# Down projections of a two-layer decoder step: activation sums made in the up projections and streamed, contraction split by even and odd blocks

## The chip, the cores and the metric

The kernel runs on one core of one Trainium2 chip. The metric is the device time of one execution in microseconds (us), the median of several runs. Instructions go to five engines: TensorE (PE, its weight loads PEld), VectorE (DVE), ScalarE (ACT), GpSimd (POOL) and SyncE (SP, whose queue SPq issues nearly all DMAs).

## The reference, cut to what matters

Two layers, each a mixer followed by a SwiGLU feed-forward block with a residual and a LayerNorm; 1088 tokens (1024 of a prompt, 64 samples), all in float32. The part that the change touches:

```python
D_MODEL = 1024; D_FF = 2816
def swiglu(x, w_gu, w_down):
    gate, up = jnp.split(x @ w_gu, 2, axis=-1)
    return (jax.nn.silu(gate) * up) @ w_down
# in each layer
x = layer_norm(ALPHA * x + swiglu(x, w_gu, w_down), g, b)
```

## The kernel before, in words

Every float32 product is made of three matmuls of rounded parts: ACT casts an operand to its high part, DVE subtracts to get the low part, and PE multiplies high by high, high by low and low by high.

**Up projection, `ffn_up`.** `KF` = 22 iterations `j`, one for each block of 128 of the 2816 hidden channels. Each iteration makes seven products of a 2x2 block scheme (`PRODUCTS`), in two halves of 272 tokens. The weights of `j + 1` need four sums ("T sums", `make_t_sums`, L2179), which POOL makes first in iteration `j`; ACT casts them (`w_part`) and DVE makes the low parts. After the fourth product (`S_T2`) ACT must copy the PSUM bank away (`take`, L2251), before PE may start the fifth, `S_T3`, which uses the same bank. ACT's order within an iteration is written out by hand: copy of the first product, casts of B11 and B21, the SiLU of the first gate, casts of T1 and T2, `take` of `S_T2`, and so on. POOL ends an iteration with the two products that give the activations: `u3` (tokens from 544) and `u2` (tokens 0 to 543). SP stores both to `scratch_a` (L2196, L2198), and then issues the two 512 KB weight loads of `j + 2` (L2187).

**Down projection, `ffn_down`.** The 22 blocks are cut into a first and a second half of 11 (`KH2`), the prompt's tokens into two halves of 512, the 1024 outputs into two of 512. Seven products `p` of 11 steps `k` each (77 steps `n`); a step multiplies one 128x512 activation operand by one 128x512 weight operand with 12 matmuls (4 token tiles by 3 parts), and in products 0, 1, 4 and 5 two more for the sample tokens. `FACTOR_A` and `FACTOR_B` say which sums are the operands: 5 of 7 products have a sum of two activation blocks, 5 of 7 a sum of two weight blocks. All activations are held on chip in `aT`. POOL makes all weight sums (L2524); the activation sums (L2533) are made by POOL, or by DVE in every second step where both are sums. Operands pass through rings: `RW` = 3 raw weights, `RS` = 2 activation sums, `RB` = 5 high and low parts. DVE also adds each finished tile of PSUM into the residual `X` (`take`, L2776 and L2780), for product `p - 1` after step 3 of product `p`, and does the LayerNorm's vector part. PE may use a PSUM bank again only when that add is done. In layer 0 the result is also transposed on PE for the next projection (L2635).

Both projections run twice: tiles `ffn0u`, `ffn0d` in layer 0, `ffn1u`, `ffn1d` in layer 1.

Of the kernel before, what the change touches and what calls it, by code (L numbers as in the profile page):

```python
# [2113 lines left out]

def ffn_up(nc, st, w, tag, q, side):
    S_B11, S_B21, S_T1, S_T2, S_T3, S_T4, S_B22 = range(7)
    X_A11, X_A12, X_S1, X_S2, X_S3, X_A22, X_S4 = range(7)
    w_v = w.rearrange("(k p) n -> p k n", p=P)
    with ExitStack() as ctx:
# [12 lines left out]
        x1, sg2 = sb("x1", [P, HALF_T]), sb("sg2", [P, HALF_T])  # L2132
        ps = ctx.enter_context(nc.psum_tensor(f"{tag}_ps", [P, 6, 512], F32))
# [4 lines left out]
        xhi_done, xlo_done = [sem(f"xhi{o}") for o in range(7)], [sem(f"xlo{o}") for o in range(7)]  # L2138
        s1_made, s2_made, s3_made, s4_made = (sem(n) for n in ("s1_made", "s2_made", "s3_made", "s4_made"))
# [40 lines left out]

        with nc.Block() as block:
# [51 lines left out]
            def _(act):  # L2233
# [46 lines left out]
                for j in range(KF):  # L2280
# [127 lines left out]
    return a_out[1]  # L2408


def ffn_down(nc, st, A, l, tag, aT, XT, y_out, a_out):
    KH2, HT, HN, RB, RW, RS, TAIL = KF // 2, SEQ // 2, D // 2, 5, 3, 2, 3
    S_BANK, UP_FREE = 7, 7
    A11, A12, A21, A22 = (0, 0), (0, 1), (1, 0), (1, 1)
    B11, B12, B21, B22 = (0, 0), (0, 1), (1, 0), (1, 1)
# [20 lines left out]
    a_sum_steps = [n for n in range(STEPS) if len(FACTOR_A[n // KH2]) > 1]  # L2436
    a_sum_at = {n: r for r, n in enumerate(a_sum_steps)}

    def dve_sums_a(n):
        return n in a_sum_at and n in w_sum_at and n % KH2 % 2 == 0  # L2440

    a_sum_count, made = {}, {True: 0, False: 0}
    for n in a_sum_steps:
        made[dve_sums_a(n)] += 1
        a_sum_count[n] = made[dve_sums_a(n)]
# [24 lines left out]
    with ExitStack() as ctx:  # L2470
        sb = lambda n, s, d=F32: ctx.enter_context(nc.sbuf_tensor(f"{tag}_{n}", s, d))
        sem = lambda n: st.sem(f"{tag}_{n}")
        X, raw, a_sum = sb("X", [P, TILES, D]), sb("w", [P, RW, HN]), sb("a_sum", [P, RS, HT])
# [8 lines left out]
        a11_in = [sem(f"a11_in{k}") for k in range(KH2)]  # L2482
        GROUPS12, GROUPS2 = [(0, 2), (2, 5), (5, 8), (8, 11)], [(0, 4), (4, 8), (8, 11)]
        a12_in, a22_in, a21_in = ([sem(f"{n}_in{g}") for g in range(len(gs))] for n, gs in
                                  (("a12", GROUPS12), ("a22", GROUPS2), ("a21", GROUPS2)))
        s_in = [sem(f"s_in{h}") for h in range(2)]
        x_first, x_right, x_left0, x_left1, x_sample = (sem(n) for n in ("x_first", "x_right", "x_left0", "x_left1", "x_sample"))
        w_sum_done, a_sum_pool, a_sum_dve = sem("w_sum_done"), sem("a_sum_pool"), sem("a_sum_dve")
# [5 lines left out]
        def a_block(ab, k):  # L2494
            h, kh = ab
            return aT[:, kh * KH2 + k, HT * h:HT * h + HT]

        def b22(k):
            return aT[:, k, HT:SEQ]

        def group_sem(sems, groups, k):
            return next(sems[g] for g, (k0, k1) in enumerate(groups) if k0 <= k < k1)

        def wait_block(eng, ab, k):
            if ab == A11:
                eng.wait_ge(a11_in[k], 16)
            elif ab == A12:
                eng.wait_ge(group_sem(a12_in, GROUPS12, k), 16)
            elif ab == A22:
                eng.wait_ge(group_sem(a22_in, GROUPS2, k), 16)  # L2510
            else:
                eng.wait_ge(group_sem(a21_in, GROUPS2, k), 16)

        def w_source(n):
            return b22(n % KH2) if FACTOR_B[n // KH2] == (B22,) else raw[:, raw_at[n] % RW, :]

        def a_source(n):
            return a_sum[:, a_sum_at[n] % RS, :] if n in a_sum_at else a_block(FACTOR_A[n // KH2][0], n % KH2)

        def sum_w(eng, op, n):  # L2520
            slot, f = raw_at[n] % RW, FACTOR_B[n // KH2]
            eng.wait_ge(w_in[slot], w_in_count[n])
            second = raw2[:, pair_at[n] % 2, :] if n in pair_at else b22(n % KH2)
            op.tensor_tensor(raw[:, slot, :], raw[:, slot, :], second, f[1]).then_inc(w_sum_done, 1)  # L2524

        def sum_a(eng, op, n, done):
            u, k = a_sum_at[n], n % KH2
            x, sign, y = FACTOR_A[n // KH2]
            wait_block(eng, x, k)
            wait_block(eng, y, k)  # L2530
            if u >= RS:
                eng.wait_ge(a_split, a_sum_steps[u - RS] + 1)
            op.tensor_tensor(a_sum[:, u % RS, :], a_block(x, k), a_block(y, k), sign).then_inc(done, 1)  # L2533
# [4 lines left out]
        with nc.Block() as block:  # L2538
            @block.sync
            def _(sp):  # L2540
                def load_group(sems, groups, g, ab):
                    k0, k1 = groups[g]
                    r = ab[1] * KH2
                    sp.dma_start(aT[:, r + k0:r + k1, HT * ab[0]:HT * ab[0] + HT],
                                 st.a_dram[r + k0:r + k1, :, HT * ab[0]:HT * ab[0] + HT].rearrange("k p t -> p k t")).then_inc(sems[g], 16)

                def load_x(i0, i1, c, landed):
                    sp.dma_start(X[:, i0:i1, HN * c:HN * c + HN],
                                 st.x_dram[i0 * P:i1 * P, HN * c:HN * c + HN].rearrange("(i p) c -> p i c", p=P)).then_inc(landed, 16)

                def load_s(h):
                    sp.dma_start(aT[:, h * KH2:(h + 1) * KH2, SEQ:NTOK],
                                 st.a_dram[h * KH2:(h + 1) * KH2, :, SEQ:NTOK].rearrange("k p t -> p k t")).then_inc(s_in[h], 16)

                for n in range(STEPS):
                    p, k = divmod(n, KH2)
                    if n == UP_FREE:
                        sp.wait_ge(a_out, 32 * (KF // 2))
                        load_s(1)
                    if n in raw_at:  # L2560
# [3 lines left out]
                        for q, (kh, ch) in enumerate(raw_pieces(p)):  # L2564
# [3 lines left out]
                            sp.dma_start(to, w_v[:, kh * KH2 + k, HN * ch:HN * ch + HN]).then_inc(w_in[r % RW], 16)  # L2568
                        if p == 0:
                            sp.dma_start(b22(k), w_v[:, KH2 + k, HN:D]).then_inc(w_in[r % RW], 16)  # L2570
                    if p == 0:
                        sp.dma_start(aT[:, k, 0:HT], st.a_dram[k][:, 0:HT]).then_inc(a11_in[k], 16)
                        if k == 0:
                            load_s(0)
                        if k == KH2 - 2:
                            load_x(0, 1, 1, x_first)
                            load_x(4, 5, 1, x_first)
                    if n == KH2 - 1:
                        for g in range(len(GROUPS12)):
                            load_group(a12_in, GROUPS12, g, A12)  # L2580
                        load_x(1, 4, 1, x_right)
                        load_x(5, 8, 1, x_right)
                        for g in range(len(GROUPS2)):
                            load_group(a22_in, GROUPS2, g, A22)
                        load_x(0, 4, 0, x_left0)
                        sp.dma_start(X[0:NS, NT, :], st.x_dram[SEQ:NTOK, :]).then_inc(x_sample, 16)
# [1205 lines left out]
```

## Time and profile before

| | |
|---|---|
| median of 3 runs | 3269.45 us (3268.17 to 3278.3) |
| the profiled execution's own time | 3274.18 us |
| its span, first to last instruction | 3272.5 us |
| PE busy | 2939.8 us, 90% of the span |
| DVE, ACT, POOL busy | 1775.2, 1204.3, 1040.3 us |
| mean granted TensorE clock | 0.932 |
| first matmul of `ffn0u` / `ffn0d` / `ffn1u` / `ffn1d` | 1166.0 / 1659.3 / 2494.8 / 2986.7 us |

The profile is of one execution. It gives busy time and counts by engine, groups of like instructions, who waited for whom, and every instruction in order of time. A matmul's shown duration overlaps the next one's; the distance of their starts is what counts. "Granted clock" is TensorE's clock as a share of 2.4 GHz.

### The profile page before, as it was taken

What the parts mean: (1) busy time and instruction counts of PE and PEld (TensorE: products, weight loads), DVE (VectorE), ACT (ScalarE), POOL (GpSimd) and SP (SyncE); (2) the same over time, 40 slices, a digit from 0 to 9 for tenths busy, and PEclk for the clock granted to TensorE, in tenths of its full rate; (3) what the DMA queues carried; (4) which work ended last, traced back from release to release, by engine and by line L of the source; (5) the groups of instructions that cost most, each with busy time, mean ns of one, the idle gap of its engine ahead of it and who ended that gap; (6) DMA issues with size and microseconds to landing.
All of it is one profiled execution on the core that took longest, in us unless ns stands there. A gap on an engine that the chain in (4) does not pass through costs nothing. (4 is left out here: it accounts for less than half of the span.)

```text
span 3272.5 us, 50986 instructions
## 1 busy us (share of the span) xinstructions
PE 2939.8 (90%) x18874; PEld 2460.4 (75%) x18893; DVE 1775.2 (54%) x3186; ACT 1204.3 (37%) x2655; POOL 1040.3 (32%) x1097
## 2 busy tenths in 40 slices
PE   7999999678999869999989969869996999998995
PEld 7889777354566569999977759836664999997784
DVE  2168443484898463333359873324546333334988
ACT  2222543433555443333333441114444333333342
POOL 2200222440111024444346534400001444443555
PEclk8999887788999989999999979959998999999998
DMA  4211102443110022222173432230001222226343
GB/s 124 74 41 42 27 27 76 135 125 101 48 39 27 20 65 80 80 80 80 54 244 105 162 103 40 66 112 23 27 27 53 79 80 80 80 67 207 120 160 119
DMA packets 269998, 269.61 MB, mean 82 GB/s; under 512 B 61779, under 2 KB 197158, under 8 KB 269734
## 3 DMA queue, kind: packets, MB, share of 16 engines
q1 hardware_dynamic: 263254, 255.57, 25.1%
q0 software_dynamic: 6512, 10.89, 1.1%
q8 instruction: 151, 2.47, 0.3%
q14 instruction: 81, 0.66, 0.1%
HBM read 212.24 MB, written 55.89 MB: 82 GB/s over the span
## 5 line engine op out<-in xcount | busy, mean ns | idle before, releaser
L2228 PE MATMUL ffn0u_ps<-ffn0u_x_hi,ffn0u_whi 128*128 128x272 f32 x1232 | 358.8, 291 | 20.4 <-DVE ffn0u_wlo L2331 10.6
L2228 PE MATMUL ffn1u_ps<-ffn1u_x_hi,ffn1u_whi 128*128 128x272 f32 x1232 | 358.4, 291 | 20.0 <-DVE ffn1u_wlo L2331 10.9
L2228 PE MATMUL ffn0u_ps<-ffn0u_x_hi,ffn0u_wlo 128*128 128x272 f32 x1232 | 356.4, 289 | 0.0
L2228 PE MATMUL ffn1u_ps<-ffn1u_x_hi,ffn1u_wlo 128*128 128x272 f32 x1232 | 356.2, 289 | 0.0
L221 PE MATMUL ine_ps<-ine_w_hi,ine_x_hi 128*128 128x256 f32 (+2 forms) x864 | 262.0, 303 | 5.2 <-DVE ine_w_lo L237 5.0
L2228 PEld LDWEIGHTS ffn0u_ps<-ffn0u_x_hi,ffn0u_whi 128*128 128x128 f32 x1232 | 234.6, 190 | 22.5 <-DVE ffn0u_wlo L2331 21.2
L2228 PEld LDWEIGHTS ffn1u_ps<-ffn1u_x_hi,ffn1u_whi 128*128 128x128 f32 x1232 | 234.2, 190 | 22.2 <-DVE ffn1u_wlo L2331 20.9
L221 PE MATMUL ine_ps<-ine_w_hi,ine_x_lo 128*128 128x256 f32 (+2 forms) x864 | 249.4, 289 | 0.0
L221 PE MATMUL ine_ps<-ine_w_lo,ine_x_hi 128*128 128x256 f32 (+2 forms) x864 | 248.9, 288 | 0.0
L2228 PEld LDWEIGHTS ffn0u_ps<-ffn0u_x_hi,ffn0u_wlo 128*128 128x128 f32 x1232 | 234.4, 190 | 0.0
L2228 PEld LDWEIGHTS ffn1u_ps<-ffn1u_x_hi,ffn1u_wlo 128*128 128x128 f32 x1232 | 234.4, 190 | 0.0
L2228 PE MATMUL ffn0u_ps<-ffn0u_q,ffn0u_whi 128*128 128x272 f32 x704 | 202.5, 288 | 0.0
L2228 PE MATMUL ffn1u_ps<-ffn1u_q,ffn1u_whi 128*128 128x272 f32 x704 | 202.5, 288 | 0.0
L221 PEld LDWEIGHTS ine_ps<-ine_w_hi,ine_x_hi 128*128 128x128 f32 (+1 forms) x864 | 166.4, 193 | 15.9 <-issue 8.5
L221 PEld LDWEIGHTS ine_ps<-ine_w_hi,ine_x_lo 128*128 128x128 f32 (+1 forms) x864 | 166.4, 193 | 4.1 <-issue 4.1
L221 PEld LDWEIGHTS ine_ps<-ine_w_lo,ine_x_hi 128*128 128x128 f32 (+1 forms) x864 | 166.2, 192 | 0.0
L2228 PE MATMUL ffn0u_ps<-ffn0u_e,ffn0u_whi 128*128 128x272 f32 x528 | 154.7, 293 | 0.0
L2228 PE MATMUL ffn1u_ps<-ffn1u_e,ffn1u_whi 128*128 128x272 f32 x528 | 154.6, 293 | 0.0
L2604 PE MATMUL ffn0d_ps<-ffn0d_w_hi,ffn0d_a_hi 128*128 128x512 f32 x308 | 125.2, 407 | 24.1 <-DVE ffn0d_X L2780 11.7
L2604 PE MATMUL ffn1d_ps<-ffn1d_w_hi,ffn1d_a_hi 128*128 128x512 f32 x308 | 124.5, 404 | 24.4 <-DVE ffn1d_X L2780 11.7
L3343 POOL TENSOR_TENSOR odd_X<-odd_X,odd_gb 128x1024 f32<-128x1024 f32 (+1 forms) x9 | 21.2, 2352 | 358.6 <-ACT odd_X L3304 358.6
L2228 PEld LDWEIGHTS ffn0u_ps<-ffn0u_q,ffn0u_whi 128*128 128x128 f32 x704 | 132.6, 188 | 0.0
(559 smaller groups left out, 7902.5 us busy)
## 6 DMA issues: line engine op xcount, KB each, us to landing
ffn0u_raw<-in_ffn_w_gu_dram SPq DMA_DIRECT2D x44, 512.0 KB, 5.1
ffn0d_w<-in_ffn_w_down_dram SPq DMA_DIRECT2D x88, 256.0 KB, 2.9
ffn1u_raw<-in_ffn_w_gu_dram SPq DMA_DIRECT2D x44, 512.0 KB, 5.4
ffn1d_w<-in_ffn_w_down_dram SPq DMA_DIRECT2D x88, 256.0 KB, 3.0
scratch_a<-ffn0u_u SPq DMA_DIRECT2D x44, 272.0 KB, 2.1
scratch_a<-ffn1u_u SPq DMA_DIRECT2D x44, 272.0 KB, 2.1
aT<-scratch_a SPq DMA_DIRECT2D x8, 1024.0 KB, 10.8
aT<-scratch_a SPq DMA_DIRECT2D x10, 768.0 KB, 9.2
```

The source lines that it names most:

```text
L221: last = nc.tensor.matmul(o, xp[:, k, i * P:i * P + r], wp[:, g % RING, 0:n], start=(k == 0 and j == 0 and i % 2 == 0), stop=(k == KD - 1 ...
L2228: last = nc.tensor.matmul(ps[:, bank + h, 0:TOK2], wp, xp, start=(begins and k == 0 and n == 0), stop=(k == KH - 1 and n == 2), skip_group ...
L2604: last = nc.tensor.matmul(ps[:, bank(p, t), :], ap[:, n % RB, t * P:t * P + P], wp[:, n % RB, :], start=(k == 0 and j == 0), stop=(k == KH ...
L3343: nc.gpsimd.tensor_tensor(X[0:r, j % 4, :], X[0:r, j % 4, :], gb[0:r, 1, :], ALU.add).then_inc(norm_done, 1)
```

## The change

Blocks are paired as (0,1), (2,3), ..., (20,21) instead of (0,11), (1,12), ...: even blocks are one half of the contraction and odd ones the other. The two blocks of a pair are now made by neighbouring iterations of `ffn_up`, and there POOL makes the five activation sums of each of the first ten pairs, in pieces of 128x256 through a ring of three (`pair`), from which SP stores them to `scratch_pairs`. The sums of the eleventh pair are made in `ffn_down` by POOL (5 "late" sums). `ffn_down` loads one 128x512 activation operand for each step into a ring of 4, plain or already summed, and neither holds `aT` nor sums activations otherwise. `RW` goes from 3 to 4 and `RB` from 5 to 6. Token halves are now 0 to 543 and 544 to 1087, so the prompt's tiles 4 to 7 start at token 544 and the small last tile consists of tokens 512 to 543 and 1056 to 1087; outputs, residual loads and the copies of the transposes follow that.

```diff
 def ffn_up(nc, st, w, tag, q, side):
+    CR, CW = 3, 256
+    PARTS = HALF_A // CW
+        pair = sb("pair", [P, CR, CW])
...
             def _(sp):
+                def store_pair(i):
+                    for c in range(len(A_SUMS)):
+                        for h in range(PARTS):
+                            m = pair_uses(i, c) + h
+                            sp.wait_ge(pair_made, m + 1)
+                            sp.dma_start(st.pair_dram[c, i, :, CW * h:CW * h + CW], pair[:, m % CR, :]).then_inc(pair_out[m % CR], 16)
                 for j in range(KF):
                     if j + 2 < KF:
                         sp.wait_ge(lo_done, 7 * (j + 1))
                         load(j + 2)
+                    if j >= 2 and j % 2 == 0:
+                        store_pair(j // 2 - 1)
                     sp.wait_ge(prod2, 2 * (j + 1))
...
             def _(act):
                     if j >= 2:
                         act.wait_ge(a_out[j % 2], 32 * (j // 2))
+                    if j >= 2:
+                        pool_pair = j // 2 - 1
+                        act.wait_ge(pair_made, pair_uses(pool_pair, 3 if j % 2 == 0 else len(A_SUMS)))
                     if j >= 1:
                         take(j, S_T2, u2[:, j % 2, :])
...
             def _(pool):
+                def pair_sum(i, c):
+                    (hx, kx), sign, (hy, ky) = A_SUMS[c]
+                    x, y = (u2, u3)[hx][:, kx, :], (u2, u3)[hy][:, ky, :]
+                    if c == 0:
+                        pool.wait_ge(prod1, 4 * i + 4)
+                    for h in range(PARTS):
+                        m = pair_uses(i, c) + h
+                        if m >= CR:
+                            pool.wait_ge(pair_out[m % CR], 16 * (m // CR))
+                        nc.gpsimd.tensor_tensor(pair[:, m % CR, :], x[:, CW * h:CW * h + CW], y[:, CW * h:CW * h + CW],
+                                                sign).then_inc(pair_made, 1)
                 for j in range(KF):
+                    if j >= 2 and j % 2 == 0:
+                        for c in range(4):
+                            pair_sum(j // 2 - 1, c)
                     if j + 1 < KF:
                         make_t_sums(pool, nc.gpsimd, j + 1)
+                    if j >= 2 and j % 2 == 0:
+                        pair_sum(j // 2 - 1, 4)
...
-    KH2, HT, HN, RB, RW, RS, TAIL = KF // 2, SEQ // 2, D // 2, 5, 3, 2, 3
+    KH2, HT, HN, RB, RW, RA, TAIL = KF // 2, HALF_A, D // 2, 6, 4, 4, 3
...
+                def load_s(kh):
+                    src = st.a_dram.rearrange("(k two) p t -> two p k t", two=2)
+                    for q, (t0, t1) in enumerate(tokens(NT)):
+                        sp.dma_start(s_raw[:, kh, :, q * NS // 2:(q + 1) * NS // 2], src[kh][:, :, t0:t1]).then_inc(s_in[kh], 16)
...
+                def load_a(n):
+                    p, k = divmod(n, KH2)
+                    f = FACTOR_A[p]
+                    if n in late_at:
+                        return
+                    if n >= RA:
+                        sp.wait_ge(a_split, n - RA + 1)
+                    if len(f) == 1:
+                        h, kh = f[0]
+                        src = st.a_dram[2 * k + kh][:, h * HALF_T:h * HALF_T + HT]
+                    else:
+                        src = st.pair_dram[A_SUMS.index(f), k]
+                    sp.dma_start(a_raw[:, n % RA, :], src).then_inc(a_in[n % RA], 16)
...
             def _(pool):
                 for n in range(STEPS):
                     if n in w_sum_at:
-                        sum_w(pool, nc.gpsimd, n)
-                    if n in a_sum_at and not dve_sums_a(n):
-                        sum_a(pool, nc.gpsimd, n, a_sum_pool)
+                        slot, sign = raw_at[n] % RW, FACTOR_B[n // KH2][1]
+                        second = raw2[:, pair_at[n] % 2, :] if n in pair_at else b22[:, n % KH2, :]
+                        pool.wait_ge(w_in[slot], w_in_count[n])
+                        nc.gpsimd.tensor_tensor(raw[:, slot, :], raw[:, slot, :], second, sign).then_inc(w_sum_done, 1)
+                    if n in late_at:
+                        (hx, kx), sign, (hy, ky) = FACTOR_A[n // KH2]
+                        pool.wait_ge(last_in, 64)
+                        pool.wait_ge(a_split, n - RA + 1)
+                        nc.gpsimd.tensor_tensor(a_raw[:, n % RA, :], a_last[:, hx, kx, :], a_last[:, hy, ky, :],
+                                                sign).then_inc(late_done, 1)
...
             def _(dve):
+                dve.wait_ge(a_out, 32 * (KF // 2))
                 for n in range(STEPS):
-                    if n + 1 < STEPS and dve_sums_a(n + 1):
-                        sum_a(dve, nc.vector, n + 1, a_sum_dve)
```

## Rows read from the trace of the kernel before

**Rows 1.** Stages: length, busy PE, PEld, DVE, ACT, POOL, clock, DMA share, GB/s.

```profile
1190.00:1650.00 460.00, 453.95 (x3596) 453.12 (x3594) 178.72 (x287) 158.88 (x359) 194.69 (x172) 0.99 0.24 73
...
1696.80:1735.90 39.10, 36.95 (x155) 29.32 (x154) 33.32 (x37) 13.87 (x24) 21.88 (x16) 0.96 0.44 146
1735.90:1767.30 31.40, 31.40 (x135) 24.81 (x134) 30.46 (x33) 11.67 (x20) 19.92 (x14) 1.00 0.44 146
1767.30:1805.90 38.60, 32.06 (x133) 26.04 (x132) 35.83 (x38) 14.43 (x26) 25.64 (x16) 0.91 0.40 135
1805.90:1841.00 35.10, 35.10 (x155) 28.30 (x154) 23.60 (x30) 13.01 (x23) 17.11 (x13) 1.00 0.58 197
...
1876.20:1927.50 51.30, 40.66 (x177) 32.06 (x176) 49.82 (x64) 20.12 (x36) 27.36 (x16) 0.87 0.31 110
```

**Rows 2.** Waits of PE in `ffn0d`: us in total, times, longest.

```profile
PE ffn0d_ps L2604 <- DVE ffn0d_X L2780: 11.7, 2, 6.5
...
PE ffn0d_ps L2604 <- DVE ffn0d_X L2776: 2.2, 1, 2.2
```

**Rows 3.** PE in order of time around the longer wait: start, duration.

```profile
1776.05 0.80 PE L2604 MATMUL ffn0d_ps<-ffn0d_w_hi,ffn0d_a_hi 128*128 128x512 f32 x1 [6.54 <-DVE ffn0d_X L2780]
...
1777.07 0.63 PE L2604 MATMUL ffn0d_ps<-ffn0d_w_lo,ffn0d_a_hi 128*128 128x512 f32 x1
1777.49 0.63 PE L2604 MATMUL ffn0d_ps<-ffn0d_w_hi,ffn0d_a_hi 128*128 128x512 f32 x1
...
1780.05 0.39 PE L2604 MATMUL ffn0d_ps<-ffn0d_w_hi,ffn0d_a_hi 128*128 128x512 f32 x1
1780.28 0.40 PE L2604 MATMUL ffn0d_ps<-ffn0d_w_hi,ffn0d_a_lo 128*128 128x512 f32 x1
```

**Rows 4.** Groups in `ffn0d`: busy us, mean ns, idle before.

```profile
L2828 DVE TENSOR_TENSOR ffn0d_a_lo<-ffn0d_a_sum,ffn0d_a_hi 128x512 fp32r<-128x512 f32 x55 | 65.5, 1191 | 0.3
...
L2533 DVE TENSOR_TENSOR ffn0d_a_sum<-aT 128x512 f32<-128x512 f32 x18 | 21.4, 1188 | 2.1
```

**Rows 5.** DVE alone, splits of product 3 and of product 4.

```profile
1761.00:1797.60 36.60, 35.52 (x36) 0.91 0.30 95
1797.60:1829.80 32.20, 23.55 (x27) 1.00 0.74 253
```

**Rows 6.** DVE in order of time: first add of the last product.

```profile
1917.82 0.66 DVE L2780 TENSOR_TENSOR ffn0d_X<-ffn0d_X,ffn0d_ps 128x512 f32<-128x512 f32 x1
```

**Rows 7.** POOL in order of time, around the turn of an iteration of `ffn0u`.

```profile
1397.12 0.78 POOL L2322 TENSOR_TENSOR ffn0u_u<-ffn0u_u,ffn0u_x 128x272 f32<-128x272 f32 x1 [0.73 <-DVE ffn0u_u L2358]
1397.86 1.29 POOL L2179 TENSOR_TENSOR ffn0u_wlo_full<-ffn0u_raw 128x512 f32<-128x512 f32 x1
1399.29 1.30 POOL L2179 TENSOR_TENSOR ffn0u_wlo_full<-ffn0u_raw,ffn0u_wlo_full 128x512 f32<-128x512 f32 x1
```

**Rows 8.** ACT in order of time, same iteration.

```profile
1403.94 1.12 ACT L2240 CAST ffn0u_whi<-ffn0u_wlo_full 128x512 fp32r<-128x512 f32 x2
1407.11 0.39 ACT L2251 COPY ffn0u_u<-ffn0u_ps 128x272 f32<-128x272 f32 x1 [2.05 <-PE ffn0u_ps L2228]
1408.55 0.39 ACT L2251 COPY ffn0u_u<-ffn0u_ps 128x272 f32<-128x272 f32 x1 [1.05 <-PE ffn0u_ps L2228]
```

**Rows 9.** SP's queue in order of time, at 544 us and in that iteration.

```profile
544.24 1.42 SPq L657 DMA_DIRECT2D ine_stage<-in_state_gla_dram  x2
...
1398.31 1.20 SPq L2187 DMA_DIRECT2D ffn0u_raw<-in_ffn_w_gu_dram  x2
```

**Rows 10.** DMA issues: a store alone (1394.8 us); the second load (1398.8 us).

```profile
scratch_a<-ffn0u_u SPq DMA_DIRECT2D x1, 272.0 KB, 2.0
ffn0u_raw<-in_ffn_w_gu_dram SPq DMA_DIRECT2D x1, 512.0 KB, 5.7
```

**Rows 11.** DMA issues, 545.6 to 546 us: two neighbours in the queue.

```profile
ine_stage<-in_state_gla_dram SPq DMA_DIRECT2D x1, 512.0 KB, 7.5
scratch_h<-H SPq DMA_DIRECT2D x1, 332.0 KB, 7.7
```

More of the change, by code:

```diff
@@ L2435, in ffn_down, with tokens @@
     w_sum_at = {n: r for r, n in enumerate(w_sum_steps)}
[L2436 to L2445, printed above, removed]
+    late_steps = [n for n in range(KH2 - 1, STEPS, KH2) if len(FACTOR_A[n // KH2]) > 1]
+    late_at = {n: r for r, n in enumerate(late_steps)}
+    a_in_count, got = {}, [0] * RA
+    for n in range(STEPS):
+        got[n % RA] += 0 if n in late_at else 16
+        a_in_count[n] = got[n % RA]
+    def tokens(i):
+        if i < NT:
+            t0 = i * P if i < NT // 2 else HALF_T + (i - NT // 2) * P
+            return [(t0, t0 + P)]
+        return [(HT, HALF_T), (HALF_T + HT, NTOK)]
     w_in_count, landed = {}, [0] * RW
@@ L2492, in ffn_down @@
         t_done, t_copied, dch, stored = sem("transposed"), sem("copied"), sem("dve_step"), sem("stored")
[L2494 to L2512, printed above, removed]
-        def w_source(n):
[L2515 to L2533, printed above, removed]
+        def w_source(n):
+            return b22[:, n % KH2, :] if FACTOR_B[n // KH2] == (B22,) else raw[:, raw_at[n] % RW, :]
         def bank(p, t):
@@ L2578, in _ @@
[L2578 to L2586, printed above, removed]
@@ L2599, in _ @@
+                    for t0, t1 in tokens(i):
+                        for u, m, y in y_out(t0, t1):
+                            sp.dma_start(y, X[r + u:r + u + m, i, :]).then_inc(stored, 16)
+                        r += t1 - t0
+                sp.wait_ge(stored, 16 * sum(len(y_out(t0, t1)) for i in NORM_ORDER for t0, t1 in tokens(i)))
             @block.tensor
@@ L2696, in copy_t @@
                     for h in range(2):
-                        j, r = 2 * ln.pos[i] + h, rows(i)
+                        j = 2 * ln.pos[i] + h
                         act.wait_ge(t_done, j + 1)
-                        nc.scalar.copy(XT[:, 4 * h:4 * h + 4, i * P:i * P + r],
-                                       ps[:, j % 2, :].rearrange("p (k t) -> p k t", k=4)[:, :, 0:r]).then_inc(t_copied, 1)
+                        u = 0
+                        for t0, t1 in tokens(i):
+                            last = nc.scalar.copy(XT[:, 4 * h:4 * h + 4, t0:t1],
+                                                  ps[:, j % 2, :].rearrange("p (k t) -> p k t", k=4)[:, :, u:u + t1 - t0])
+                            u += t1 - t0
+                        last.then_inc(t_copied, 1)
                 act.wait_ge(a_out, 32 * (KF // 2))
@@ L3618, in rest, with y_rows @@
 def rest(nc, st, A, C, O, hT, hs):
-    def y_rows(i):
-        if i < NT:
-            return O[0][0, i * P:(i + 1) * P, :]
-        return O[1].rearrange("b s d -> (b s) d")
-    XT, place = even_end(nc, st, A, hT, hs, lambda i: st.x_dram[i * P:i * P + rows(i), :])
+    def y_rows(t0, t1):
+        both = ((0, SEQ, O[0][0]), (SEQ, NTOK, O[1].rearrange("b s d -> (b s) d")))
+        cuts = ((max(t0, a), min(t1, b), a, y) for a, b, y in both)
+        return [(u0 - t0, u1 - u0, y[u0 - a:u1 - a, :]) for u0, u1, a, y in cuts if u0 < u1]
+    XT, place = even_end(nc, st, A, hT, hs, lambda t0, t1: [(0, t1 - t0, st.x_dram[t0:t1, :])])
     hs = ExitStack()
```

146 lines of the change are left out of this document (76 added, 70 removed).

## The prediction, made before the changed kernel was run

> **What bounds the kernel now.** I read the page first (PE busy for 90% of the span), then stages, PE's waits, and then each engine in order of time. In the up projection PE is busy for 454 of 460 us at a clock of 0.99 [rows 1]: it is bound by PE, and DVE (179), ACT (159) and POOL (195) only have to hand things over in time. In the down projection it depends on the product. Product 4 (with sample matmuls) runs with PE full in 35.1 us, product 2 (without) in 31.4; but product 1, of product 4's size, takes 39.1, and product 3, of product 2's size, 38.6 with DVE busy for 35.8 [rows 1]. PE waits there for DVE's adds into `X`: 2.2 us once and 6.5 + 5.2 us [rows 2]. After such a wait TensorE runs at its lower level of 1.2 GHz for a while: after the 6.5 us its matmuls start 0.42 us apart (1777.07, 1777.49), from 1780.05 on 0.23 apart [rows 3]. Nine matmuls to 1780.05 took 4.0 us and would have taken 2.1, so a stall costs about 1.9 us more than its own length. That is needed twice below.
>
> **The down projections: what is removed.** Per layer DVE loses 18 activation sums, 21.4 us [rows 4], and POOL 37 of the 55 less 5 late ones. DVE also slows where POOL works: its low parts of summed activations take 1191 ns in the mean [rows 4]. Where POOL makes only weight sums, as the changed kernel's POOL nearly always does, DVE is busy for 23.6 us in the splits of a product (product 4, its 4 adds of 2.5 us included: 21.1 without); in product 3, 35.5 [rows 5]. With its 8 adds of about 0.6 (4.9 us) product 3 would cost DVE 21.1 + 4.9 = 26 us, under PE's 31.4. So DVE stops being late: product 1 goes from 39.1 to 35.1 (-4.0), product 3 from 38.6 to 31.4 or a bit less (-7.5), and the last product loses its wait of 5.2 with the slow clock behind it, 1.9 (-7.1). The deeper rings (`RB` 6, `RW` 4) help the same way. In the tail, what ends last is a chain on DVE: the first add of the last product starts at 1917.82 [rows 6], then four tiles of adds, statistics and scaling follow. Product 6 starts at 1876.2 [rows 1] and now at about 1864.7; PE needs some 31 us for it and finishes its first tile 6 us before the end, with 2 us of transposes between: 1864.7 + 31 - 6 + 2 = 1891.7 against 1917.82, so the tail moves by about 26 us, the 18.6 above included. I take 25 to leave room for what is added: activations are now loaded step by step, 256 KB in 2.7 to 3.2 us, 80 to 95 GB/s more than the 135 to 197 GB/s of the middle products [rows 1]; the sample's activations come in rows of 128 bytes; and the second raw weight still has only two slots. Bounds: 17 us per layer (the three waits and their slow clock are 19.6, less 3 for the start), 31 (all of product 6's surplus). Both layers: **-50**, from -34 to -62. The late sums (5 per layer) lie in POOL's free time. Two DMAs more for the last rows and the split copies cost under 1 us.
>
> **The up projections: what is added.** In every even iteration from 2 on, ten per layer, POOL first makes eight pieces (c = 0 to 3), then the T sums, then two more pieces. Work alone is small. A 128x272 operation takes 0.78 us and a 128x512 one 1.29 [rows 7], so a piece takes 0.74; eight are 5.9 us. POOL has the time: it is busy for 195 of 460 us. What counts is when the T sums come. POOL's last product of the iteration before ends at 1397.9 and T2 is ready at 1399.29 + 1.30 = 1400.6 [rows 7]. ACT casts T1 and T2 at 1403.94, and only behind them, at 1407.11, copies the first half of `S_T2`'s bank [rows 8]. PE needs that copy when it has ended the second half, at 1408.55 [rows 8]. So T2 may be late by 7 us or so; then ACT stands at its cast, the copies queue behind it, and PE stops.
>
> Now the ring of three. Piece 3 may start only when piece 0's store has landed. SP issues the two weight loads (1 MB) at 1398.31, for 1.20 us [rows 9], and only then the stores, from 1399.6 on. A 272 KB store alone lands in 2.0 us; the second load lands 5.7 us after its issue at about 1398.8, at 1404.5 [rows 10]. Does a store behind a load wait for it? At 545.7 us, just behind two loads issued over 544.24 to 545.66 [rows 9], a 332 KB store took 7.7 us instead of 2.0, like the load ahead of it with 7.5 [rows 11]: it landed about 0.9 us after that one. So the queue passes nothing. The Trainium skill ("DMA: Bandwidth & Descriptors", Queues, rings and completion order) says why: a DMA's semaphore increment lands only after every earlier write of that DMA engine. By that rule, the trace agrees, the sum is the one below; by the same page's fit for a lone DMA (2.0 us + bytes / 436 GB/s, 2.3 us for 128 KB) it would be that of the first rival, an estimate of +32 us here in place of +122.
>
> Worked out, with the two loads landing 1.6 us apart, 128 KB takes 0.4: pieces 0 to 2 are made by 1400.1 and land at 1404.9, 1405.3, 1405.7. Pieces 3 to 5 are made one after another, to 1405.7, 1406.4, 1407.1. Piece 6 needs piece 3's store, now alone in the queue: 1405.8 + 1.8 = 1407.6 (the 2.0 of 272 KB, a little less for half the size); it ends at 1408.3. Piece 7 ends at 1409.1. T2 is then ready 2.7 us on, at 1411.8 instead of 1400.6; the cast (0.6) and the copy (0.39) end at 1412.8. PE has stood since 1408.55: **4.2 us**. Behind it come 1.9 us for the slow clock (taken from [rows 3]; this wait lies between 2.2 and 6.5, after both of which the clock was low). 6.1 us in 20 iterations: **+122**. What is late next is `S_T3` and all behind it; the odd iteration after it starts its T sums at once and loses nothing. Bounds per iteration: 3.6 us with the slow clock at 0 (84 with 4.2), and 7.4 (4.9 + 2.5) if the stores land another 0.4 us later each: +84 to +148.
>
> **Sum.** 122 - 50 = +72 us. The profiled execution took 3274.2 us beside its span of 3272.5; so 3346 for it, and from the median of 3269.45, 4.7 below it, **3342 us**. The likeliest case's own range: 84 - 62 = +22 to 148 - 34 = +114, so 3291 to 3383.
>
> **Rivals.**
> First, stores don't wait for the loads (faster). Then piece 0's store lands at 1399.6 + 2.0 = 1401.6, pieces 3 to 5 end by 1403.8, piece 3's store lands at 1404.4, piece 7 ends at 1405.9, T2 at 1408.6, the copy at 1409.6: PE stands for 1.0 us, too short for any wait after which the trace shows the low clock. 20 x 1.0 - 50 = -30: 3239. For it speaks that the middle of an iteration leaves the DMA engines idle; against it [rows 11]. It turns faster when an even iteration costs under 2.5 us: that is when piece 0 lands before about 1403. 0.17.
> Second, the stall is there but the clock stays up: 84 - 50 = +34: 3303. Against it [rows 3]. 0.10.
> Third, the down projections gain nothing, because each step now hangs on its own load behind those of weights and of `X` (in product 0 the DMA engines are full already), and a step late there costs what DVE's lateness did: +122, 3391. For it: waits of POOL for weights; against it: 135 to 197 GB/s in the middle products, and loads issued four steps, 11 us, ahead. 0.06.
> The likeliest case: 0.67.
>
> **How the numbers follow.** A difference of 0.3% (10 us) is about what a measurement of this kernel can tell from none. Faster: the first rival, less its edge: 0.16. Same: what lies between it and the others: 0.03. Slower: the rest, 0.81. The range is 3275 to 3390: it takes in the second rival and the likeliest case's range, reaches below for a ring that waits less than worked out, and leaves out most of the first rival and the end of the third.
>
> **What the changed profile would show.** Right: PE's waits in both up projections for ACT's copy (L2251 before, at `S_T3`), 10 per layer of some 4 us, a granted clock of about 0.9 there, the stage some 60 us longer per layer; POOL idle before a piece, ended by a DMA to `scratch_pairs`; that DMA at over 4 us to landing for the first three of a pair. In the down projections no wait of PE for DVE's `X` in the products 1, 3 and 6, and DVE busy for 60 us less. Wrong: pair stores landing in 2 us right behind loads, or PE full through the up projection, or waits for activations in the down projection. The prediction fails first if ACT's cast of T2 is not what stands before the copy, or if the stall is so spread that the clock stays up.

## The result

The changed kernel takes 3344.48 us (median of 5 runs, 3335.7 to 3349.09) against 3269.45 (5 runs): the ratio is 1.022, 95% interval 1.0199 to 1.024. It is slower by 75 us; forecast were 3342 us and slower. In the two profiled executions (the span grows from 3272.5 to 3342.9, by 70.4) the time lies where the prediction had put it. From the first matmul of `ffn0u` to that of `ffn0d` it is 552.0 us where it was 493.4, and in layer 1 550.3 where it was 491.9: +117.0. From the first matmul of `ffn0d` to that of the next stage it is 269.9 where it was 293.3, and from that of `ffn1d` to the end 262.2 where it was 285.8: -47.0.

Stages of the changed kernel, with the columns of [rows 1]: the steady part of `ffn0u`, then products 1, 3 and 4 of `ffn0d`.

```profile
1210.00:1635.00 425.00, 384.79 (x2934) 383.07 (x2934) 149.22 (x226) 134.21 (x299) 218.74 (x227) 0.95 0.31 95
1756.46:1792.59 36.13, 35.45 (x156) 28.24 (x154) 29.61 (x38) 13.72 (x25) 12.91 (x9) 1.00 0.62 181
...
1823.75:1853.67 29.92, 29.92 (x133) 24.78 (x132) 27.00 (x31) 12.57 (x22) 17.37 (x12) 1.00 0.77 248
1853.67:1888.79 35.12, 35.12 (x156) 28.32 (x154) 19.35 (x28) 12.60 (x22) 6.55 (x5) 1.00 0.62 200
```

In 425 us of the up projection PE is now idle for 40, at a clock of 0.95. In the down projection product 3 has gone from 38.6 to 29.9 us, with DVE busy for 27.0 of them instead of 35.8, and PE is full at clock 1.00; products 1 and 4 now take 36.1 and 35.1.

Waits of PE, first in `ffn0u`, then in `ffn0d` (total, times, longest):

```profile
PE ffn0u_ps L2251 <- ACT ffn0u_u L2274: 41.0, 10, 5.4
...
PE ffn0d_ps L2632 <- DVE ffn0d_X L2814: 0.7, 1, 0.7
```

The waits of 11.7 and 2.2 us for `X` in [rows 2] are down to 0.7. New are ten waits for ACT's copy in `ffn0u`; `ffn1u` has ten as well, of 40.0 us in all. Here is one of them, POOL of the changed kernel in order of time:

```profile
1278.04 2.13 POOL L2347 TENSOR_TENSOR ffn0u_pair<-ffn0u_u 128x256 f32<-128x256 f32 x3
1285.38 2.13 POOL L2347 TENSOR_TENSOR ffn0u_pair<-ffn0u_u 128x256 f32<-128x256 f32 x3 [5.20 <-DMA scratch_pairs<-ffn0u_pair]
1287.91 1.41 POOL L2347 TENSOR_TENSOR ffn0u_pair<-ffn0u_u 128x256 f32<-128x256 f32 x2 [0.40 <-DMA scratch_pairs<-ffn0u_pair]
1289.28 1.26 POOL L2191 TENSOR_TENSOR ffn0u_wlo_full<-ffn0u_raw 128x512 f32<-128x512 f32 x1
1290.69 1.26 POOL L2191 TENSOR_TENSOR ffn0u_wlo_full<-ffn0u_raw,ffn0u_wlo_full 128x512 f32<-128x512 f32 x1
```

ACT in order of time, in the same iteration:

```profile
1290.65 0.62 ACT L2263 CAST ffn0u_whi<-ffn0u_wlo_full 128x512 fp32r<-128x512 f32 x1 [7.06 <-POOL ffn0u_wlo_full L2191]
1292.06 0.62 ACT L2263 CAST ffn0u_whi<-ffn0u_wlo_full 128x512 fp32r<-128x512 f32 x1 [0.79 <-POOL ffn0u_wlo_full L2191]
1292.59 0.67 ACT L2274 COPY ffn0u_u<-ffn0u_ps 128x272 f32<-128x272 f32 x2
```

And PE:

```profile
1293.11 0.57 PE L2251 MATMUL ffn0u_ps<-ffn0u_x_hi,ffn0u_whi 128*128 128x272 f32 x1 [4.52 <-ACT ffn0u_u L2274]
1293.47 0.43 PE L2251 MATMUL ffn0u_ps<-ffn0u_q,ffn0u_whi 128*128 128x272 f32 x1
...
1295.74 0.37 PE L2251 MATMUL ffn0u_ps<-ffn0u_x_hi,ffn0u_wlo 128*128 128x272 f32 x1
1295.94 0.29 PE L2251 MATMUL ffn0u_ps<-ffn0u_x_hi,ffn0u_whi 128*128 128x272 f32 x1
1296.08 0.29 PE L2251 MATMUL ffn0u_ps<-ffn0u_q,ffn0u_whi 128*128 128x272 f32 x1
```

Read from the bottom up, it is the chain of the prediction: PE waits 4.5 us for the copy; the copy stands behind ACT's cast of T2; the cast waits for POOL's T sum; the T sum stands behind the eight pieces; and piece 3 waits for piece 0's store, until 7.3 us after the first piece's start (1278.04 to 1285.38). Forecast were 7.0 us for that and 4.2 us for PE's wait. Then the matmuls start 0.23 us apart to 1295.74 rather than 0.13. SP's queue (start, duration) shows what stood ahead of that store, and the DMA issues of 1278.0 to 1281.3 us how long they took to land:

```profile
1278.38 1.91 SPq L2208 DMA_DIRECT2D ffn0u_raw<-in_ffn_w_gu_dram  x2
1280.33 16.71 SPq L2205 DMA_DIRECT2D scratch_pairs<-ffn0u_pair  x10
```

```profile
ffn0u_raw<-in_ffn_w_gu_dram SPq DMA_DIRECT2D x2, 512.0 KB, 5.1
scratch_a<-ffn0u_u SPq DMA_DIRECT2D x1, 272.0 KB, 2.8
scratch_pairs<-ffn0u_pair SPq DMA_DIRECT2D x1, 128.0 KB, 5.0
```

The store's own data comes late, and not only the word of it. Its packets are of 1024 bytes and those of the two weight loads of 512, so the trace tells them apart. In the 18 even iterations with a load, the first store packet starts 3.4 to 3.8 us after the store's issue, when 86 to 95% of the loads' packets have started; where no load is ahead, it starts 0.8 us after the issue and the store lands in 1.7.

One count was wrong, and the trace of the changed kernel tests the mechanism by it. In the last even iteration, 20, there is no weight load left to issue. POOL there:

```profile
1667.26 2.13 POOL L2347 TENSOR_TENSOR ffn0u_pair<-ffn0u_u 128x256 f32<-128x256 f32 x3
1669.80 3.79 POOL L2347 TENSOR_TENSOR ffn0u_pair<-ffn0u_u 128x256 f32<-128x256 f32 x4 [0.41 <-DMA scratch_pairs<-ffn0u_pair]
1673.98 0.74 POOL L2347 TENSOR_TENSOR ffn0u_pair<-ffn0u_u 128x256 f32<-128x256 f32 x1 [0.39 <-DMA scratch_pairs<-ffn0u_pair]
```

The same work on the same engines: piece 3 starts 2.5 us after the first instead of 7.3, and PE then waits 0.8 us. So 18 iterations stall, not 20.

### The profile page after: what moved, and what is told of

Same layout as the page of the kernel before. It is cut to its first block and busy times, and to the rows that moved or that the text cites. A ratio compares the mean times of both kernels' runs of the same rounds, so it can differ in the third digit from the quotient of the medians.

```text
span 3342.9 us, 51347 instructions
## 1 busy us (share of the span) xinstructions
PE 2959.2 (89%) x18874; PEld 2483.1 (74%) x18893; DVE 1718.3 (51%) x3150; ACT 1203.7 (36%) x2657; POOL 1082.3 (32%) x1233
## 5 line engine op out<-in xcount | busy, mean ns | idle before, releaser
L2251 PE MATMUL ffn0u_ps<-ffn0u_x_hi,ffn0u_whi 128*128 128x272 f32 x1232 | 367.5, 298 | 61.2 <-ACT ffn0u_u L2274 41.0
L2251 PE MATMUL ffn1u_ps<-ffn1u_x_hi,ffn1u_whi 128*128 128x272 f32 x1232 | 367.4, 298 | 60.2 <-ACT ffn1u_u L2274 40.0
L2251 PEld LDWEIGHTS ffn0u_ps<-ffn0u_x_hi,ffn0u_whi 128*128 128x128 f32 x1232 | 242.1, 196 | 65.3 <-issue 43.6
L2251 PEld LDWEIGHTS ffn1u_ps<-ffn1u_x_hi,ffn1u_whi 128*128 128x128 f32 x1232 | 242.0, 196 | 64.3 <-issue 42.7
L2251 PEld LDWEIGHTS ffn0u_ps<-ffn0u_x_hi,ffn0u_wlo 128*128 128x128 f32 x1232 | 241.8, 196 | 0.0
L2251 PEld LDWEIGHTS ffn1u_ps<-ffn1u_x_hi,ffn1u_wlo 128*128 128x128 f32 x1232 | 241.8, 196 | 0.0
L2376 DVE TENSOR_TENSOR ffn0u_wlo<-ffn0u_wlo_full,ffn0u_whi 128x512 fp32r<-128x512 f32 x88 | 79.5, 923 | 147.9 <-POOL ffn0u_wlo_full L2191 100.5
L2376 DVE TENSOR_TENSOR ffn1u_wlo<-ffn1u_wlo_full,ffn1u_whi 128x512 fp32r<-128x512 f32 x88 | 79.5, 924 | 146.5 <-POOL ffn1u_wlo_full L2191 99.3
L2251 PEld LDWEIGHTS ffn1u_ps<-ffn1u_q,ffn1u_whi 128*128 128x128 f32 x704 | 140.4, 199 | 0.0
L2251 PEld LDWEIGHTS ffn0u_ps<-ffn0u_q,ffn0u_whi 128*128 128x128 f32 x704 | 140.2, 199 | 0.0
```

Of the source, the lines that this page charges most:

```text
L2251: last = nc.tensor.matmul(ps[:, bank + h, 0:TOK2], wp, xp, start=(begins and k == 0 and n == 0), stop=(k == KH - 1 and n == 2), skip_group ...
L2376: nc.vector.tensor_tensor(w_lo[:, j % 2, s, :, :], weight(j, s), w_hi[:, j % 2, s, :, :].bitcast(F32), ALU.subtract).then_inc(lo_done, 1)
```

## The experiments

All ratios below are to the kernel before, run on the same chip; their 95% intervals stand in brackets. Each time is a median of 4 to 10 runs. "Steady part" is 1210 to 1635 us, which holds the nine stalls of `ffn0u`; there the kernel before has PE busy for all of the 425 us.

### Up projection: the order in SP's queue (e1_stores_first)

```diff
+                    if j >= 2 and j % 2 == 0:
+                        store_pair(j // 2 - 1, 0, 4)
                     if j + 2 < KF:
                         sp.wait_ge(lo_done, 7 * (j + 1))
                         load(j + 2)
                     if j >= 2 and j % 2 == 0:
-                        store_pair(j // 2 - 1)
+                        store_pair(j // 2 - 1, 4, 5)
```

`store_pair(i, c0, c1)` stores the pieces of the sums `c0` to `c1 - 1`; the lines that give it these arguments are left out here.

> SyncE now issues the stores of the pieces of c = 0 to 3 ahead of the two weight loads (the last two pieces still behind them); nothing else is changed. My theory (the ring of three stalls because a store lands only behind the 1 MB loads ahead of it in the queue): piece 0's store lands about 2 us after its issue, an even iteration costs 0 to 1.0 us over the 21.05 of before, as the last even iteration of each up projection (which has no load ahead) costs 1.0 to 1.7, and the time is about 3240 (3226 to 3250); the loads are issued up to 7 us later, which costs nothing as they are needed only an iteration later. Rival (the stall is the work of GpSimd, eight pieces of 0.7 us ahead of the T sums, or contention of the DMA engines with other traffic): the even iterations stay at 27 to 28 us and the time at 3344, within 10.

Measured: 3245.74 us, ratio 0.9913 (0.9896 to 0.993). Nothing but the order of eight stores and two loads in the queue is changed, and 99 us are gone: the kernel is now faster than before. PE's wait in `ffn0u` and SP's queue:

```profile
PE ffn0u_ps L2253 <- ACT ffn0u_u L2276: 10.3, 10, 2.3
```

```profile
1224.47 7.04 SPq L2205 DMA_DIRECT2D scratch_pairs<-ffn0u_pair  x8
1231.55 1.14 SPq L2208 DMA_DIRECT2D ffn0u_raw<-in_ffn_w_gu_dram  x2
```

Piece 3 now starts 2.5 to 3.4 us after the first piece in all ten turns of `ffn0u`. Ten waits of PE are left there, 1.0 us in the mean (the first rival's 1.0), one of them of 2.3. The loads are issued 7 us later, and no wait for them appears in the trace. The rival that GpSimd's work is the stall falls.

### The loads in another queue (e2_loads_on_act)

The two loads of `j + 2` are issued by ACT, between the two copies of `S_B11`'s bank, and SP's queue holds stores alone (the lines that take the loads out of SP's queue and define `load_next` are left out here):

```diff
                         nc.scalar.copy(to[:, hs(h)], ps[:, A_BANK + h, 0:TOK2]).then_inc(copied, 1)
+                        if j >= 1 and s == S_B11 and h == 0 and j + 2 < KF:
+                            load_next(j)
```

> The weight loads of the up projection are issued from ScalarE's DMA queue, at about the same time as before, so that SyncE's queue holds the stores alone. It tells whether the store waits because it stands behind the loads in one queue, or because both pass through the same 16 DMA engines. If the order within the queue is all: stores land in 2 us and the time is 3235 to 3250. If the engines share themselves out evenly between two queues: a store lands in 2.5 to 4 us, part of the stall stays, 3260 to 3300. If the load fills the engines whatever the queue (first come, first served): stores land after 6 us as now and the time is 3340 to 3350. I hold the second for the likeliest.

Measured: 3325.54 us, ratio 1.0167 (1.0143 to 1.0191). ACT's queue, SP's, and the issues of 1261.9 to 1262.4 us:

```profile
1261.55 1.84 ACTq L2278 DMA_DIRECT2D ffn0u_raw<-in_ffn_w_gu_dram  x2
...
1262.16 10.12 SPq L2205 DMA_DIRECT2D scratch_pairs<-ffn0u_pair  x8
```

```profile
ffn0u_raw<-in_ffn_w_gu_dram ACTq DMA_DIRECT2D x2, 512.0 KB, 7.1
scratch_pairs<-ffn0u_pair SPq DMA_DIRECT2D x1, 128.0 KB, 5.5
```

This store has no load ahead of it in its queue, only the 272 KB store that is ahead of it in every kernel; the two loads are issued 0.6 and 0.2 us before it in the other queue. It still takes 5.5 us. It is one of the slower ones: of the 18 first stores of a pair that follow loads, the profile tells the landing of 12, and they took 4.1 to 6.1 us, 4.3 at the median. In the changed kernel 12 such landings took 5.0 to 5.5, 5.2 at the median. The first packet now starts 2.6 to 3.2 us after the issue, when 37 to 46% of the loads' packets have started, so the packets of the two queues do mix, and the store gains a little by it. That is not enough: the starts of PE's matmuls stand 3.7 to 5.6 us apart in each even iteration up to 18. I had held the second case for likelier; the time lies between what the second and the third would give, and about 19 us of the 99 come back. So another queue is no way out here, where the load is issued first. Why a store whose packets mix with the loads' lands so late is open.

### The work without the stores (e3_not_stored)

```diff
-                    if j >= 2 and j % 2 == 0:
-                        store_pair(j // 2 - 1)
...
                         if m >= CR:
-                            pool.wait_ge(pair_out[m % CR], 16 * (m // CR))
+                            pool.wait_ge(pair_made, m - CR + 1)
...
-                        src = st.pair_dram[A_SUMS.index(f), k]
+                        src = st.a_dram[2 * k, :, 0:HT]
```

> The pieces are made as before, but not stored, and a piece waits for no store; the down projections load blocks of the plain activations in place of the sums (same bytes), so the outputs are not those of the reference. The work of GpSimd is whole and its wait is gone. My theory: eight pieces of 0.70 us end 5.6 us after the first, T2 is ready 8.3 us after it, which ScalarE's copy can bear without PE waiting: an even iteration takes 21.05 to 21.4 us and the time is 3344 - 18 x 6.5 - 2 x 1.3 = 3224 (3218 to 3232). Rival (GpSimd's work is the delay): 3300 or more. The difference from the kernel with the stores ahead of the loads is what the stores' own 2 us cost in a ring of three.

Measured: 3221.97 us, ratio 0.9843 (0.982 to 0.9865). Steady part:

```profile
1210.00:1635.00 425.00, 425.00 (x3389) 424.90 (x3388) 182.14 (x262) 151.48 (x340) 256.13 (x257) 1.00 0.24 73
```

All of the pieces are made, POOL is busy for 256 us, and PE never waits. The up projections take 483.4 and 483.9 us from first to last matmul, against 482.9 and 481.8 before the change. So the sums' work costs them next to nothing, and the stall comes from waiting for the stores.

### What the clock adds (e4_filler)

```diff
+    FILL = 34
...
                         pe.wait_ge(lo_done, 7 * j + s + 1)
+                        if s == S_T3 and j >= 2 and j % 2 == 0 and j + 2 < KF:
+                            for _ in range(FILL):
+                                nc.tensor.matmul(ps[:, 6, 0:TOK2], w_hi[:, j % 2, s, 0, :], x_hi[:, x, 0, hs(0)], start=True,
+                                                 stop=True, skip_group_check=True)
```

> In the even iterations 2 to 18 PE does 34 dummy matmuls of 272 columns into an unused bank (3.9 us at full clock) just before the first matmul of S_T3, where it now stands still for 4 to 5.6 us. Outputs are unchanged. If the slow matmuls behind the stall come from PE having stood still (the prediction took 1.9 us for them), the clock stays at its upper level and each of the 18 iterations gains 1.5 to 2.3 us: 3344 - 18 x 1.9 = 3310 (3303 to 3317). Rival (the slow clock costs nothing here, or comes for another reason): 3344, within 6, or later by what of the dummy work sticks out.

Measured: 3310.01 us, ratio 1.0111 (1.0089 to 1.0134): PE does more work, and 34 us are gained on the changed kernel. Steady part:

```profile
1210.00:1635.00 425.00, 421.92 (x3347) 421.04 (x3346) 157.67 (x236) 137.47 (x308) 227.66 (x234) 1.00 0.31 97
```

The clock is 1.00 where the changed kernel has 0.95. In the changed kernel, the low clock follows each of the nine stalls of `ffn0u`, for 12 to 27 matmuls, and the distances of their starts sum to about 16.4 us more than at the upper level: 1.8 us per stall, where the prediction took 1.9 from [rows 3].

### GpSimd's order alone, and with the queue's (e9_split_alone, e8_first_and_split)

```diff
-                        for c in range(4):
+                        for c in range(3):
                             pair_sum(j // 2 - 1, c)
-                    if j + 1 < KF:
+                        make_t_sums(pool, nc.gpsimd, j + 1, 0, 2)
+                        pair_sum(j // 2 - 1, 3)
+                        make_t_sums(pool, nc.gpsimd, j + 1, 2, 4)
+                    elif j + 1 < KF:
                         make_t_sums(pool, nc.gpsimd, j + 1)
```

`make_t_sums` takes the first and the last of the sums that it makes as two more arguments (those lines are left out here). e9 is this with the loads ahead of the stores as in the changed kernel:

> GpSimd's order alone is changed (pieces of c = 0 to 2, T1, T2, pieces of c = 3, T3, T4, pieces of c = 4); the weight loads stay ahead of the stores. My theory: pieces 0 to 2 are stored behind the loads as now and pieces 3 to 5 wait for them until 7.3 us, but T2 no longer waits for piece 3's store and two more pieces: it is ready at 9.4 + 2.6 = 12.0 us instead of 13.9 after the first piece, so PE waits 2.5 us instead of 4.4, and the slow clock behind it may stay: 18 x 1.9 = 34 us less, 3310 (3300 to 3322). Rival (the ring is not what holds the T sums): 3344. The gain of the kernel with both changes then is the loads' place in the queue for the larger part.

e8 is this with the diff of the first experiment too:

> The stores of c = 0 to 3 go ahead of the weight loads, and GpSimd makes the pieces of c = 0 to 2, then T1 and T2, then those of c = 3, then T3 and T4, then c = 4. My theory: T2 comes 2 pieces (1.4 us and a wait) sooner than with the stores ahead alone, so that PE waits nowhere in the even iterations: 21.05 us each, 3344 - 18 x 6.5 - 2 x 1.3 = 3224 (3219 to 3232), 45 us below the kernel before. Rival (T3 and T4 come too late in their turn, or the later loads make the T sums of the next iteration wait): 3235 to 3260.

Measured: e9 3285.31 us, ratio 1.0047 (1.0027 to 1.0067); e8 3218.44 us, ratio 0.9845 (0.9821 to 0.987). Steady part of e9, then of e8:

```profile
1210.00:1635.00 425.00, 401.63 (x3151) 399.78 (x3150) 158.06 (x243) 141.29 (x319) 234.81 (x241) 0.99 0.32 99
```

```profile
1210.00:1635.00 425.00, 425.00 (x3394) 425.00 (x3393) 171.36 (x258) 152.98 (x339) 257.71 (x256) 1.00 0.33 103
```

e8 stores everything and has PE full: the up projections take 482.9 and 481.8 us from first to last matmul, as before (482.9, 481.8), and the gain of the down projections is left whole. It beats the kernel before by 1.5%.

e9 gained 59 us where I had expected 34. The waits are shorter, as worked out: 23.4 us in nine in `ffn0u` instead of 40.2 (41.0 less the 0.8 of iteration 20). What I had left out is that a shorter wait can end without the low clock. Two of e9's waits, PE in order of time:

```profile
1281.41 0.36 PE L2251 MATMUL ffn0u_ps<-ffn0u_x_hi,ffn0u_whi 128*128 128x272 f32 x1 [2.88 <-ACT ffn0u_u L2274]
...
1282.37 0.34 PE L2251 MATMUL ffn0u_ps<-ffn0u_q,ffn0u_whi 128*128 128x272 f32 x1
1282.50 0.43 PE L2251 MATMUL ffn0u_ps<-ffn0u_x_hi,ffn0u_wlo 128*128 128x272 f32 x1
1282.73 0.43 PE L2251 MATMUL ffn0u_ps<-ffn0u_x_hi,ffn0u_whi 128*128 128x272 f32 x1
...
1327.94 0.28 PE L2251 MATMUL ffn0u_ps<-ffn0u_x_hi,ffn0u_wlo 128*128 128x272 f32 x1
1328.06 0.29 PE L2251 MATMUL ffn0u_ps<-ffn0u_x_hi,ffn0u_whi 128*128 128x272 f32 x1
```

Behind the wait of 2.88 us the starts go from 0.13 to 0.23 us apart; behind the next one, in which the starts stand 2.63 us apart, they stay at 0.13. Six of e9's nine waits in `ffn0u` were followed by no low clock at all, and five of nine in `ffn1u`.

### Down projection: what had made VectorE late

Five kernels bring back parts of what the changed kernel no longer does. The sums in e6, e7, e10 and e11 are dummy work into a buffer that nobody reads. e5 sets `RB` and `RW` back:

```diff
-    KH2, HT, HN, RB, RW, RA, TAIL = KF // 2, HALF_A, D // 2, 6, 4, 4, 3
+    KH2, HT, HN, RB, RW, RA, TAIL = KF // 2, HALF_A, D // 2, 5, 3, 4, 3
```

> The rings of the down projection go back from 6 and 4 slots to 5 and 3; all else is as in the changed kernel. If the gain of 48 us in the down projections comes from VectorE and GpSimd doing less (as the prediction has it, with the rings as a help), 0 to 6 us are lost: 3344 to 3350. Rival (the deeper rings bring it by riding over the same lateness): products 3 and 6 wait for X or for weights again and 20 us or more are lost: 3364 and up.

e6 gives GpSimd its sums again:

```diff
+                    if was_summed(n) and not dve_summed(n) and n not in late_at:
...
+                        nc.gpsimd.tensor_tensor(junk[:, :], a_last[:, 0, 0, :], a_last[:, 1, 0, :], ADD).then_inc(junked, 1)
```

> GpSimd does again the 32 activation sums that it had in each down projection, of 128x512 elements, but as dummy work into a buffer that nobody reads; outputs are unchanged. If contention of VectorE with GpSimd is what made VectorE late before, the splits of summed activations take 1.2 us in the mean again rather than about 1.0, PE waits in product 3 and 6, and 10 to 25 us of the gain are lost: 3354 to 3369. If VectorE's own sums were the load that mattered: 0 to 5 us lost, 3344 to 3349. I expect the first in its lower half, as VectorE has room now.

e7 gives VectorE its own:

```diff
+                    if n + 1 < STEPS and dve_summed(n + 1):
...
+                        nc.vector.tensor_tensor(junk[:, :], a_last[:, 0, 0, :], a_last[:, 1, 0, :], ADD).then_inc(junked, 1)
```

> VectorE does again its 18 activation sums in each down projection (21 us per layer), as dummy work into a buffer that nobody reads, each ahead of its step's split; outputs are unchanged. VectorE's own load as the cause: in product 3 six more operations of 1.1 us make 26 + 6.6 = 33 us against PE's 30 to 31, so that it is late there again by 2 to 3 us and product 6 by as much: 5 to 15 us over both layers, 3350 to 3360. Both loads were then needed for the lateness of before. Rival (VectorE's sums alone did it): 30 us or more lost, 3374 and up. Other rival (the rings or the loads did it): 3344 to 3347.

e11 has the edits of e6 and e7 together, e10 those of e5, e6 and e7:

> Both kinds of activation sums of the down projection come back as dummy work, GpSimd's 32 and VectorE's 18 per layer, with the deep rings of the changed kernel; outputs are unchanged. Alone they cost 9 to 16 us and nothing. If lateness only shows when VectorE's own load and the slower operations beside GpSimd add up (product 3: 26 + 6.6 us and a fifth more per split against PE's 30), this costs far more than the sum: product 3 back at 36 to 38.6 us, product 6 at 45 to 51, 3375 to 3390. If the two are independent: their sum, 3353 to 3360.

> As the kernel with both kinds of dummy sums, and the rings at 5 and 3 slots as well: all that the prediction credits with the gain of the down projections is taken back, while activations are still streamed and sums still come from DRAM. If that is all of the cause, the down projections lose the 48 us again: 3385 to 3400. What is missing from 48 is due to something not named (the held activations, the order of loads). With independent costs (8 + 13 + 0): 3365.

The seven products from the first matmul of product 0 to the end of the last of product 6, in us; the last column adds both layers. In e1, e2, e4, e8 and e9, whose down projections are those of the changed kernel, both layers together take 477.2 to 479.4 us (changed: 479.4), so a difference of 2 us says nothing.

| kernel | time | ratio | `ffn0d` | `ffn1d` | against the changed kernel |
|---|---|---|---|---|---|
| changed | 3344.48 | 1.022 | 243.1 | 236.4 | |
| before | 3269.45 | 1 | 268.2 | 257.8 | +46.5 |
| e5, rings | 3352.09 | 1.0266 (1.0234 to 1.0297) | 251.6 | 240.5 | +12.6 |
| e6, GpSimd's sums | 3360.17 | 1.0288 (1.0257 to 1.0319) | 255.3 | 243.1 | +19.0 |
| e7, VectorE's sums | 3341.36 | 1.023 (1.02 to 1.026) | 247.7 | 236.4 | +4.6 |
| e11, both sums | 3386.19 | 1.0351 (1.0314 to 1.0389) | 265.9 | 254.5 | +41.0 |
| e10, all three | 3403.19 | 1.0415 (1.038 to 1.045) | 277.6 | 265.9 | +64.0 |

Product 3 in e6, in e7 and in e11, each in a fence of its own:

```profile
1816.35:1846.83 30.48, 30.25 (x134) 24.70 (x132) 30.34 (x30) 11.75 (x22) 21.95 (x15) 1.00 0.65 207
```

```profile
1813.84:1845.28 31.44, 30.21 (x133) 24.70 (x132) 27.78 (x35) 11.53 (x20) 18.21 (x11) 1.00 0.65 205
```

```profile
1833.25:1868.95 35.70, 31.83 (x133) 25.87 (x132) 32.61 (x37) 12.65 (x22) 26.78 (x17) 0.95 0.61 197
```

Beside GpSimd's dummy sums alone VectorE is busy for all of the product and yet only just in time; with its own sums alone it has 3.7 us to spare; with both it is busy for 32.6 us, PE waits, and the clock falls. The waits of [rows 2] are back in e11's `ffn0d`, 4.1 us in product 1, 3.9 in product 3 and 3.5 in product 6:

```profile
PE ffn0d_ps L2641 <- DVE ffn0d_X L2835: 7.3, 2, 3.9
...
PE ffn0d_ps L2641 <- DVE ffn0d_X L2831: 4.1, 1, 4.1
```

e6 shows the contention itself, the low parts of the activations in `ffn0d`, first the changed kernel, then e6:

```profile
L2865 DVE TENSOR_TENSOR ffn0d_a_lo<-ffn0d_a,ffn0d_a_hi 128x512 fp32r<-128x512 f32 x77 | 76.8, 997 | 1.6 <-ACT ffn0d_a_hi L2712 1.6
```

```profile
L2881 DVE TENSOR_TENSOR ffn0d_a_lo<-ffn0d_a,ffn0d_a_hi 128x512 fp32r<-128x512 f32 x77 | 99.6, 1293 | 0.0
```

The same operation takes 997 or 1293 ns by what GpSimd does. The sum of e6 and e7 is 23.6 us, e11 has 41.0: the costs are not independent, and neither kind of sum alone was the cause. Two expectations missed: e7's cost was overrated (3350 to 3360 expected), and the rings' was underrated (3344 to 3350 expected, 12.6 us in the products). Both kinds of sums together take back 41.0 of the 46.5 us. e10 takes back more than all of it; its dummy sums stand at other places in the engines' order than the sums of before did, and the streamed loads remain, so what makes the 17.5 us beyond is open.

## Why the prediction was right

- **The stall of the up projections** was shown to be what it said: a 128 KB store behind 1 MB of loads, in a ring of three, ahead of the T sums (e1, e3, and iteration 20). PE stood for 3.8 to 5.4 us, 4.4 in the mean of the 18, where 4.2 were forecast, and lost 1.8 behind each in `ffn0u` where 1.9 were.
- **The count** was off: 20 iterations of 6.1 us were summed to 122; the runs have 18 of about 6.4 and two of about 1, 117.0 in all. Two errors of opposite sign: the mechanism was right, but that the total came within 5 us was partly luck. The lower bound has a slip, too: it names 3.6 us per iteration, while its 84 us are 20 times 4.2 (20 times 3.6 are 72); nothing hangs on it.
- **The low clock** as a price of its own was right (e4: 34 us for 18 iterations, 1.9 each). The second rival is thereby out. It came with each of the 18 waits of the changed kernel, but with only 7 of the 18 shorter ones of e9. The clock of the steady part was 0.95, not "about 0.9".
- **The first rival** was what the changed kernel lacks: its 1.0 us for an even iteration is what e1 measured (10.3 us in ten waits), and 3239 us is close to e1's 3245.7.
- **The queue's rule.** By the Trainium skill ("DMA: Bandwidth & Descriptors", Queues, rings and completion order) an increment lands only after every earlier write of that DMA engine, across its queues. The landings agree: 5.0 us for the store behind the loads in one queue, 4.3 at the median with the loads in another, 1.7 alone. But the prediction took the rule for the reason, and in one queue the packets show more than it says: the store's data itself starts only when the loads' data is nearly through. The fit of the same page (the Trainium skill, "DMA: Bandwidth & Descriptors", Anatomy of one DMA), which the prediction applied to SyncE's stores, is given there for DMAs that GpSimd issues; its 2.3 us for 128 KB compare with 1.7 measured.
- **The down projections**: -50 was forecast, -47.0 measured. Product 6 starts 205.5 us after product 0 instead of 216.8, so 11.3 us sooner by itself (11.5 forecast). Product 3 went to 29.9, below the 31.4, with DVE at 27.0 (26 forecast); product 1 went to 36.1 in `ffn0d`, not to 35.1. That the relief was two kinds of work acting together, as product 3's working had it (fewer operations and shorter ones), was shown by e6, e7 and e11. "The rings help the same way" was right in kind and had no size: 12.6 us of products. The third rival is out: product 0, where the streamed activations were to hurt, takes 38.0 and 38.6 us instead of 37.4 and 37.7, and the products shown above run with PE full or nearly so while 181 to 248 GB/s are moved.

## What to carry to other kernels

A small store whose landing opens a ring slot must be issued ahead of bulk loads, not behind them, and moving the loads to another queue helped little (19 us); the order in one queue was worth 99 us here. When an engine late in a chain costs PE a wait, price the wait and the slow clock behind it apart, since a shorter wait can be free of the second. And when two kinds of work have to add up to make an engine late, putting one back by itself says little: put them back one at a time and together.

## What the runs showed of the hardware

- A 128 KB store behind 1 MB of loads in the same queue took 5.0 to 5.5 us to land, and its first packet started after 86 to 95% of the loads' had. With the loads in a different queue, issued 0.6 and 0.2 us before it, it took 4.1 to 6.1 us, and its first packet started after 37 to 46% of theirs (e2). Alone it took 1.7 us.
- TensorE's clock, by the starts of matmuls in both up projections, iterations 2 to 18: at its lower level (1.2 GHz) after each of the changed kernel's 18 waits, in which the starts stand 4.1 to 5.7 us apart; after 7 of the 18 waits of 2.4 to 3.8 us in e9 (one of 2.96 among them, one of 3.65 not); in e1 after both of 2.3 and 2.6 and after none of 1.0 to 1.7. Yet in the kernel before, near the start of `ffn0u`, starts 1.76 us apart (to 1197.5) were followed by 18 slow matmuls. So the length of the wait alone does not tell. After the changed kernel's waits it stayed low for 12 to 27 matmuls of 272 columns.
- GpSimd's 128x256 sums of two operands took 0.70 us each from start to start.
- A VectorE operation of 128x512 elements took 997 ns or 1293 ns in the mean, by what GpSimd did beside it (changed kernel and e6).
